# Three rounded matmuls in place of one plain f32 matmul in two input projections, rounding moved from VectorE to ScalarE, and a triangular inverse accumulated in PSUM

## The chip, the cores and the metric

The kernel runs on one core of a Trainium2 chip. The metric is the device time of one execution in microseconds. Engines are called as in the profile: PE (TensorE), DVE (VectorE), ACT (ScalarE), POOL (GpSimd), SP (SyncE, which here only issues DMAs).

## What is computed

Four transformer layers of width 1024 over 512 tokens, all in float32, with a context of 256 tokens. Cut to the parts that the change touches:

```python
# layer 1 (diff_fourier_mixer): q, k, v, f for the tokens, k and v for the context too
kv_c = h_ctx @ w_in[:, DA_W:3 * DA_W]
q, k, v, f = jnp.split(h_lat @ w_in, [DA_W, 2 * DA_W, 3 * DA_W], axis=-1)
...
# layer 2 (hyena_mixer)
u = dwconv3(h @ w_in, conv_w, conv_b)        # w_in is 1024 x 3072
...
# layer 3 (gated delta rule, 8 heads, chunks, two directions)
sol = lax.linalg.triangular_solve(lmat, rhs, left_side=True, lower=True, unit_diagonal=True)
```

Each of layers 1 and 2 ends in a gated convolutional FFN, each of layers 3 and 4 in a mixture of experts. Layer 4 has a short convolution as its mixer. Every mixer ends in an output projection.

## The kernel before, in words

The program is a list of 48 stages (`stages`). Each engine walks the list; after each stage it drains, adds one to `stage_end` and waits until all four have done so (L2782). Work of different stages never overlaps, except that SP loads weight slabs of 2 MB ahead of time into a ring of four slots (`slab`, `load_slab`); a slab's slot is free when its last user has called `used`.

**Rounded products.** A float32 product is made of three matmuls on operands rounded to the type fp32r: high x high, high x low, low x high (`three`, L508). `high` (L494) writes a rounded copy, `low` (L499) subtracts it from the original in place. `Parts` does this for a projection: the weights come in units of 128x1024 (one tile of 128 outputs), and the source is eight slices of 128x512. Before the change DVE makes the high parts of the units and of the source, and the low parts of the source (`cut_source`), POOL the low parts of the units (`make_low`), and PE waits for both in `product`. A ring of three units holds the high parts. It is used by `Project` (four stages), `FfnIn` (two), `ShortConv` (one), and in another form, by rows, by `FfnOut` (two). The high parts of the first three units precede those of the source on DVE. The experts' stages do their rounding on ACT already.

**AttentionIn** computes q, k, k of the context, v and f, 22 tiles, by plain f32 matmuls (L658); a plain f32 matmul stands in the trace as two records. After each of tiles 1 to 8 PE turns the halves for the rotary embedding (`swap`). DVE copies the tiles out, does the rotation, and between them (`BESIDE`) sums eight slabs of a `Modulation` (a matrix-vector product, L366 and L370, with short matmuls L382 on PE). The arena columns A_V, A_P and so on share the room of the later attention.

**HyenaIn** computes 24 tiles by plain f32 matmuls (L1269). ACT takes each out of PSUM with scale and bias (L1285), DVE adds the two other taps (`conv3`) and sums 12 side slabs. **HyenaFilter**, ahead of it, loads the table `hy_fwd` into Y_TAB, where it stays for **HyenaConv**, whose PE starts on it (L1338) after 32 transposes; `hy_back` is loaded over it later (L1319).

**DeltaHeads** runs eight heads, each with two directions, called lanes, of six 128x128 blocks. For each lane it inverts a unit triangular matrix by doubling: a level v takes the mask M of that level, A = M T (PE, L1793, into PSUM), copies A to SBUF (ACT, L1884), X = A TT (PE, L1803), TT -= X (DVE, L1974), and T = the 32x32 blockwise transpose of TT (DVE, L1977). M of the next level is a DVE product (`mask`, L1933). Up to level 4 T comes by the transpose, at level 5 (`WHOLE`) by its own product, and level 6 needs TT only. Then come six scan steps, beside which PE makes the next head's projections.

Of the kernel before, what the change touches and what calls it, by code (L numbers as in the profile page):

```python
# [27 lines left out]
P = 128  # L28
# [61 lines left out]
def _constants():  # L90
# [24 lines left out]
    masks = np.stack(levels, 1).reshape(P, 14 * P).astype(np.float32)  # L115
# [376 lines left out]
def high(c, dve, out, v):  # L492

    return dve.tensor_copy(c.rounded(out), v)  # L494
# [9 lines left out]

# [5 lines left out]
class Parts:  # L512

    def __init__(self, core, room, src, count):
        self.c, self.src = core, src
        self.src_high, self.ring = core.view(room, KD, T), room + KD * T
        self.cut, self.cut0 = core.shared("parts_cut", KD)  # L520
        self.made, self.made0 = core.shared("parts_high", count)
        self.low, self.low0 = core.shared("parts_low", count)

    def unit_high(self, u):
        return self.c.view(self.ring + KD * P * (u % UNITS), KD, P)

    def cut_source(self, dve):
        for k in range(KD):
            high(self.c, dve, self.src_high[:, k, :], self.src[:, k, :])
            dve.drain()  # L530
            low(self.c, dve, self.src[:, k, :], self.src_high[:, k, :]).then_inc(self.cut, 1)

    def make_high(self, dve, u, w, full, done):

        if u >= UNITS:
            dve.wait_ge(full, done + u - UNITS + 1)
        high(self.c, dve, self.unit_high(u), w).then_inc(self.made, 1)
# [4 lines left out]

    def product(self, pe, out, u, w):
        pe.wait_ge(self.low, self.low0 + u + 1)
        for k in range(KD):
            if u == 0:
                pe.wait_ge(self.cut, self.cut0 + k + 1)
            ins = three(self.c, pe, out, self.unit_high(u)[:, k, :], w[:, k, :], self.src_high[:, k, :], self.src[:, k, :],
                        k == 0, k == KD - 1)
        return ins  # L550


class Project(Stage):


    def __init__(self, core, w, src, gate, keep, room):
# [4 lines left out]
        self.parts = Parts(core, room, src, KD)  # L561
# [11 lines left out]
    def gpsimd(self, pool):  # L573
        for m in range(KD):
            self.parts.make_low(pool, m, self.unit(m))

    def vector(self, dve):
        c = self.c

        def make_high(m):  # L580
            if m < KD:
                if m % 4 == 0:
                    c.arrived(dve, self.n[m // 4])
                self.parts.make_high(dve, m, self.unit(m), self.full, self.base)

# [2301 lines left out]
```

## Time and profile before

| | us |
|---|---|
| three runs, median (lowest to highest) | 5049.75 (5049.54 to 5050.94) |
| the profiled execution, its time | 5045.87 |
| its span, first to last instruction | 5044.0 |

Its stages, cut at the last drain of each at L2782 (start and length in us): AttentionIn 107.00, 155.5; Project 485.12, 58.2; FfnIn 598.71, 280.3; FfnOut 879.01, 130.0; HyenaFilter 1035.63, 142.2; HyenaIn 1204.47, 182.0; HyenaConv 1386.43, 134.0; Project 1520.43, 57.5; FfnIn 1633.13, 289.3; FfnOut 1922.41, 128.9; DeltaHeads 2146.78, 1125.3; Project 3272.06, 58.3; experts 3412.69, 583.5; ShortConv 4045.18, 148.8; Project 4193.99, 57.5; experts 4333.84, 656.3. PE is busy for 82% of the span, DVE for 62%, ACT for 30%, POOL for 21%. Since the stages meet, the time is the sum of their lengths, and each length is read by itself: when its first matmul starts, how fast its tiles follow each other, and what trails the last one.

### The profile page before, as it was taken

To read this page: it belongs to the slowest core of one execution; us is meant where nothing else is said; L and a number is where in the kernel's file an instruction comes from. 1 tells how busy PE (TensorE), PEld (TensorE's weight loads), DVE (VectorE), ACT (ScalarE), POOL (GpSimd) and SP (SyncE) were. 2 spreads that over 40 slices of the span, in tenths; PEclk is the share of its full clock that TensorE was granted. 3 is DMA by queue.
4 is the path that set the end of the run, shared out by engine and by line. 5 is a ranking of instruction groups with operands and counts; after the bars stand their busy time and mean duration, and the time that the engine had idled before them with its cause. 6 is when DMAs were issued, how large, how long until landed. Compare 5 with 4: busy or idle time off the path is not lost. (4 is left out here: it accounts for less than half of the span.)

```text
span 5044.0 us, 50691 instructions
## 1 busy us (share of the span) xinstructions
PE 4138.2 (82%) x18124; PEld 3086.6 (61%) x18124; DVE 3127.2 (62%) x3756; ACT 1492.9 (30%) x1740; POOL 1049.8 (21%) x482
## 2 busy tenths in 40 slices
PE   4956799968986999678788888767999687599995
PEld 2523477723444777466666766656888566488884
DVE  5554577644644977355555455637999553699995
ACT  1031211011101110222222212106777400377773
POOL 0000243400001343000000000023555232155551
PEclk9977899969998999798988899778999898799997
DMA  4310155211510452100000000009999610699993
GB/s 170 134 67 18 50 174 193 76 55 67 205 45 34 150 170 90 33 17 17 17 17 17 17 17 6 28 19 348 363 359 370 223 67 2 247 377 359 369 357 121
DMA packets 372002, 689.22 MB, mean 137 GB/s; under 512 B 38311, under 2 KB 118311, under 8 KB 371304
## 3 DMA queue, kind: packets, MB, share of 16 engines
q1 hardware_dynamic: 327696, 639.79, 35.7%
q10 hardware_dynamic: 24888, 30.89, 1.8%
q0 software_dynamic: 19296, 16.94, 1.0%
q8 instruction: 75, 1.23, 0.1%
q14 instruction: 47, 0.39, 0.0%
HBM read 697.91 MB, written 41.00 MB: 146 GB/s over the span
## 5 line engine op out<-in xcount | busy, mean ns | idle before, releaser
L508 PE MATMUL psum<-work_rounded 128*128 128x512 f32 x3328 | 1089.2, 401 | 153.6 <-DVE fixed_rounded L499 70.9
L499 POOL TENSOR_TENSOR ring_rounded<-ring,work_rounded 128x1024 fp32r<-128x1024 f32 x188 | 460.9, 2454 | 3102.7 <-DVE work_rounded L494 3102.7
L508 PEld LDWEIGHTS psum<-work_rounded 128*128 128x128 f32 x3328 | 632.7, 192 | 314.8 <-issue 171.4
L508 PE MATMUL psum<-work_rounded,fixed_rounded 128*128 128x512 f32 x2304 | 683.1, 401 | 15.3 <-DVE fixed_rounded L2600 15.3
L499 DVE TENSOR_TENSOR ring_rounded<-ring,work_rounded 128x2048 fp32r<-128x2048 f32 x256 | 585.6, 2289 | 127.6 <-ACT work_rounded L2518 123.7
L508 PE MATMUL psum<-work_rounded,ring_rounded 128*128 128x512 f32 x1504 | 598.5, 398 | 0.0
L2518 ACT ACTIVATE work_rounded<-ring 128x2048 fp32r<-128x2048 f32 x256 | 490.8, 1919 | 272.3 <-PE psum L508 171.6
L508 PEld LDWEIGHTS psum<-work_rounded,fixed_rounded 128*128 128x128 f32 x2304 | 436.1, 189 | 119.7 <-DVE ring_rounded L499 12.0
L499 DVE TENSOR_TENSOR work_rounded<-work,work_rounded 128x2048 fp32r<-128x2048 f32 (+1 forms) x196 | 435.0, 2221 | 46.7 <-ACT work_rounded L2518 37.6
L476 ACT ACTIVATE work<-fixed 128x512 f32<-128x512 f32 (+1 forms) x120 | 64.6, 595 | 1119.9 <-DVE fixed L460 769.8
L508 PE MATMUL psum<-fixed_rounded,work_rounded 128*128 128x512 f32 x960 | 381.3, 397 | 0.0
L494 DVE CAST work_rounded<-ring 128x1024 fp32r<-128x1024 f32 x188 | 166.7, 893 | 274.8 <-PE psum L508 252.9
L508 PEld LDWEIGHTS psum<-work_rounded,ring_rounded 128*128 128x128 f32 x1504 | 287.9, 191 | 66.1
L508 PE MATMUL psum<-ring_rounded,fixed_rounded 128*128 128x512 f32 x768 | 306.9, 400 | 0.0
L370 DVE SCALAR_TENSOR_TENSOR work<-ring,fixed,work 128x512 f32<-128x512 f32 x392 | 289.5, 750 | 26.1 <-issue 1.3
L1674 PE MATMUL psum<-fixed,ring 128*128 128x512 f32 (+1 forms) x768 | 299.0, 525 | 0.4 <-DVEq L2782 0.4
L2380 POOL DMA_INDIRECT pair_rows<-work x66 | 173.5, 2629 | 561.3 <-DVE work L2610 559.3
L1793 PE MATMUL psum<-work 128*128 128x128 f32 x1152 | 166.6, 300 | 139.0 <-DVEq L1961 91.7
L2518 ACT ACTIVATE work_rounded<-work 128x2048 fp32r<-128x2048 f32 x128 | 245.3, 1919 | 101.3 <-PE psum L508 83.0
L1793 PEld LDWEIGHTS psum<-work 128*128 128x128 f32 x1152 | 149.4, 207 | 155.4 <-DVEq L1961 82.7
L508 PEld LDWEIGHTS psum<-fixed_rounded,work_rounded 128*128 128x128 f32 x960 | 184.1, 192 | 40.3
L968 ACT ACTIVATE work<-psum,fixed 128x512 f32<-128x512 f32 x88 | 68.5, 779 | 465.6 <-PE psum L508 465.6
(306 smaller groups left out, 6097.7 us busy)
## 6 DMA issues: line engine op xcount, KB each, us to landing
ring<-in_w SPq DMA_DIRECT2D x128, 2048.0 KB, 12.3
work<-in_w SPq DMA_DIRECT2D x64, 2048.0 KB, 11.9
ring<-in_mod_w SPq DMA_DIRECT2D x24, 2048.0 KB, 8.9
ring<-in_ada_w SPq DMA_DIRECT2D x24, 2048.0 KB, 7.9
ring<-in_ffn_w_in SPq DMA_DIRECT2D x44, 1024.0 KB, 7.6
ring<-in_ffn_w_out SPq DMA_DIRECT2D x10, 2048.0 KB, 7.7
ring<-in_w_in_a SPq DMA_DIRECT2D x32, 512.0 KB, 6.1
ring<-in_hy_w_in SPq DMA_DIRECT2D x6, 2048.0 KB, 9.4
```

The lines of the kernel that those rows point to most:

```text
L370: ins = dve.scalar_tensor_tensor(out=acc, in0=w[:, k, :], scalar=c.par(cond, k), in1=acc, op0=ALU.mult, op1=ALU.add)
L476: act.activation(c.view(self.scratch + 512 * k, t), src[:, k, :], ACT.Square).then_inc(s["squared"], 1)
L494: return dve.tensor_copy(c.rounded(out), v)
L499: return eng.tensor_tensor(c.rounded(v), v, c.rounded(v_high), ALU.subtract)
L508: ins = pe.matmul(out, c.rounded(w), c.rounded(x), start=(start and i == 0), stop=(stop and i == 2))
L968: act.activation(buf, c.ps[:, j % 7, :], ACT.Identity, scale=c.par(f"ffn_conv_w{i}1", m), bias=c.par(f"ffn_conv_b{i}", m)).then_inc(self.c ...
L1674: ins = pe.matmul(c.ps[:, 4 + i % 4, 0:n], self.slab_dst()[:, part, k, :], src[:, k, :], start=(k == 0), stop=(k == KD - 1))
L1793: ins = pe.matmul(c.pair(4 * l, KEYS)[:, P * t:P * t + P], M[:, t, :], T_[:, t, :], start=True, stop=True)
L2380: pool.indirect_dma_start(self.c.d["pair_rows"], bass.IndirectOffsetOnAxis(ap=self.si[:, b:b + 1].bitcast(U32), axis=0), self.y_sb[:, b, : ...
L2518: act.activation(c.rounded(self.unit_high(o, u)), self.unit_raw(o, u), ACT.Copy).then_inc(self.made, 1)
```

## The change

1. **AttentionIn and HyenaIn** use three rounded matmuls per product. AttentionIn gets 16 units in a ring of four, sources of both token sets (16 slices), and the order q, k, f, v; v's weights are four units that hold two k-slices each. HyenaIn gets a ring of two units in the context's room HC0 and puts the source's high parts over Y_TAB, so HyenaConv loads `hy_fwd` anew at its start.
2. **High parts by ACT** in every stage that used `Parts`, and in FfnOut. At the start of a stage ACT makes unit 0, slices 0 and 1, unit 1, and the other slices (`open_high`); DVE makes the low parts of unit 0 and the slices (`open_low`); POOL starts with unit 1.
3. **DeltaHeads**: the masks are stored negated, TT starts in PSUM (a matmul with the identity) and X is added there (`start=False`). DVE transposes straight from PSUM; ACT copies TT out of PSUM after it (24 copies per head in place of 12).

```diff
-masks = np.stack(levels, 1).reshape(P, 14 * P).astype(np.float32)
+masks = -np.stack(levels, 1).reshape(P, 14 * P).astype(np.float32)
...
-def high(c, dve, out, v):
-    return dve.tensor_copy(c.rounded(out), v)
+def high(c, act, out, v):
+    return act.activation(c.rounded(out), v, ACT.Copy)
...
+    def open_high(self, act, first, second):
+        high(self.c, act, self.unit_high(0), first).then_inc(self.made, 1)
+        for q, (v, v_high) in enumerate(self.src):
+            if q == 2:
+                high(self.c, act, self.unit_high(1), second).then_inc(self.made, 1)
+            high(self.c, act, v_high, v).then_inc(self.raised, 1)
+
+    def open_low(self, dve, first):
+        dve.wait_ge(self.made, self.made0 + 1)
+        low(self.c, dve, first, self.unit_high(0)).then_inc(self.cut, 1)
+        for q, (v, v_high) in enumerate(self.src):
+            dve.wait_ge(self.raised, self.raised0 + q + 1)
+            low(self.c, dve, v, v_high).then_inc(self.cut, 1)
...
 class AttentionIn(Stage):
-    BESIDE = [2, 5, 8, 13, 15, 18, 19, 20]
+    BESIDE = [2, 5, 8, 12, 14, 17, 19, 20]
...
+        for u in range(2, 16):                                   # ACT
+            if u in (4, 8, 12):
+                c.arrived(act, self.n["qkfv"[u // 4]])
+            if u >= 4:
+                act.wait_ge(self.full, self.base + (u - 4 if u < 8 else u) + 1)
+            high(c, act, self.unit_high(u), self.unit(u)).then_inc(self.parts.made, 1)
...
 class HyenaIn(Stage):
+        self.parts = Parts(core, [core.h], [core.view(Y_TAB, KD, T)], 24, unit_ring(core, HC0, 2))
...
         for j, m in enumerate(self.order):                       # ACT
             act.wait_ge(self.full, self.full0 + j + 1)
+            if j + 2 < 24:
+                if (j + 2) % 4 == 0:
+                    c.arrived(act, self.n[(j + 2) // 4])
+                self.parts.make_high(act, j + 2, self.unit(j + 2), None, 0)
...
 class HyenaConv(Stage):
+        act.dma_start(self.tab, self.c.d["hy_fwd"]...).then_inc(self.table, 16)
...
 class DeltaHeads(Stage):
+        for l in range(2):                                       # PE, ahead of the levels
+            self.wait(pe, h, "mt", l + 1)
+            for t in range(NTA):
+                pe.matmul(c.pair(4 * l + 2, KEYS)[:, P * t:P * t + P], ident, self.lane(l, L_TT, NTA, P)[:, t, :],
+                          start=(t % 4 == 0), stop=True, skip_group_check=True)
...
-                    ins = pe.matmul(c.pair(4 * l, KEYS)[:, P * t:P * t + P], A[:, t, :], TT[:, t, :], start=True, stop=True)
+                    ins = pe.matmul(c.pair(4 * l + 2, KEYS)[:, cols], A[:, t, :], TT[:, t, :], start=False, stop=True,
+                                    skip_group_check=True)
...
+            for l in range(2):                                   # ACT, after the two copies of A
+                if v < WHOLE:
+                    self.wait(act, h, "upd", 2 * v + 1 + l)
+                else:
+                    self.wait(act, h, "x", 2 * v - 1 + l)
+                act.activation(self.lane(l, L_TT, KEYS), c.pair(4 * l + 2, KEYS), ACT.Copy).then_inc(s["a_out"], 1)
...
-                dve.tensor_tensor(TT, TT, ax, ALU.subtract)      # DVE
-                if v < WHOLE:
-                    dve.drain()
-                    dve.transpose(self.lane(l, L_T, KEYS), self.lane(l, L_TT, KEYS))
+                if v < WHOLE:
+                    dve.transpose(self.lane(l, L_T, KEYS), c.pair(4 * l + 2, KEYS)).then_inc(s["upd"], 1)
```

## Rows read from the trace of the kernel before

**Rows 1.** Windows by stage: busy us of each engine (instructions), granted PE clock, DMA.
```profile
107.00:262.51 155.51, 154.37 (x432) 77.19 (x432) 75.57 (x112) 0.00 (x0) 0.00 (x0) 0.99 0.33 116
1204.47:1386.43 181.96, 179.82 (x480) 83.83 (x480) 109.80 (x155) 18.65 (x24) 0.00 (x0) 0.99 0.52 187
1633.13:1922.41 289.28, 268.35 (x1184) 216.07 (x1184) 236.63 (x303) 47.32 (x67) 106.33 (x44) 0.96 0.48 163
2146.78:3272.06 1125.28, 908.37 (x5344) 742.95 (x5344) 604.58 (x1072) 235.44 (x409) 0.00 (x0) 0.89 0.06 17
```

**Rows 2.** Windows: seven units of Project (168 matmuls), three tiles of HyenaIn (48).
```profile
503.13:541.97 38.84, 38.73 (x168) 31.23 (x167) 9.62 (x13) 0.00 (x0) 12.03 (x5) 1.00 0.16 54
1213.87:1234.51 20.64, 20.64 (x49) 8.88 (x47) 10.15 (x14) 2.33 (x3) 0.00 (x0) 1.00 0.21 80
```

**Rows 3.** Timeline of the opening of the first Project: start us, us, instruction.
```profile
485.28 4.04 DVE L494 CAST work_rounded<-ring 128x1024 fp32r<-128x1024 f32 x3 [0.19 <-ACTq L2782]
486.13 7.87 POOL L499 TENSOR_TENSOR ring_rounded<-ring,work_rounded 128x1024 fp32r<-128x1024 f32 x3 [485.69 <-DVE work_rounded L494]
491.88 2.66 DVE L499 TENSOR_TENSOR fixed_rounded<-fixed,work_rounded 128x512 fp32r<-128x512 f32 x1
494.69 0.77 PE L508 MATMUL psum<-work_rounded 128*128 128x512 f32 x1 [10.33 <-DVE fixed_rounded L499]
494.96 0.69 DVE L499 TENSOR_TENSOR fixed_rounded<-fixed,work_rounded 128x512 fp32r<-128x512 f32 x1
```

**Rows 4.** Groups by line, whole kernel: busy us, mean ns, idle before.
```profile
L2518 ACT ACTIVATE work_rounded<-ring 128x2048 fp32r<-128x2048 f32 x256 | 490.8, 1919 | 272.3 <-PE psum L508 171.6 <-DMA ring<-in_w 100.7
L499 DVE TENSOR_TENSOR ring_rounded<-ring,work_rounded 128x2048 fp32r<-128x2048 f32 x256 | 585.6, 2289 | 127.6 <-ACT work_rounded L2518 123.7
L499 POOL TENSOR_TENSOR ring_rounded<-ring,work_rounded 128x1024 fp32r<-128x1024 f32 x188 | 460.9, 2454 | 3102.7 <-DVE work_rounded L494 3102.7
L2528 ACT ACTIVATE fixed_rounded<-psum 128x512 fp32r<-128x512 f32 x128 | 68.3, 586 | 0.0
L464 DVE RECIPROCAL work<-work 128x512 f32<-128x512 f32 (+1 forms) x15 | 47.1, 3139 | 100.8 <-ACT work L478 100.8
```

**Rows 5.** Groups by line and form, first FfnOut.
```profile
L499 DVE TENSOR_TENSOR work_rounded<-work,work_rounded 128x512 fp32r<-128x512 f32 x22 | 59.9, 2723 | 1.6
```

**Rows 6.** Waits of PE, first FfnIn, then second: total us, times, longest us.
```profile
PE psum L508 <- POOL ring_rounded L499: 2.3, 1, 2.3
PE psum L508 <- POOL ring_rounded L499: 5.0, 3, 2.4
```

**Rows 7.** Timeline at the start of HyenaConv (its stage begins at 1386.43).
```profile
1384.04 2.00 SPq L245 DMA_DIRECT2D ring<-in_ffn_w_in  x2
1393.14 2.41 PE L1338 MATMUL psum<-fixed,work 128*128 128x512 f32 x5 [1.27 <-DVE fixed L1356]
```

**Rows 8.** DMA issues of HyenaConv: KB each, median us to landing.
```profile
work<-in_hy_back ACTq DMA_DIRECT2D x1, 2048.0 KB, 7.7
```

**Rows 9.** Timeline of DeltaHeads: first X, one level, start of the scan.
```profile
2365.50 0.95 DVE L1974 TENSOR_TENSOR work<-work,psum 128x768 f32<-128x768 f32 x1 [0.38 <-PE psum L1803]
...
2374.79 1.60 PE L1793 MATMUL psum<-work 128*128 128x128 f32 x12 [0.79 <-DVEq L1978]
2376.43 0.81 ACT L1884 ACTIVATE work<-psum 128x768 f32<-128x768 f32 x1 [4.26 <-PE psum L1793]
2378.36 2.84 PE L1803 MATMUL psum<-work 128*128 128x128 f32 x24
2379.90 0.95 DVE L1974 TENSOR_TENSOR work<-work,psum 128x768 f32<-128x768 f32 x1 [0.38 <-PE psum L1803]
2380.93 0.98 DVE L1977 STREAM_TRANSPOSE work<-work 128x768 f32<-128x768 f32 x1
2381.99 0.49 PE L1793 MATMUL psum<-work 128*128 128x128 f32 x2 [0.79 <-DVEq L1978]
...
2406.06 0.38 PE L1815 MATMUL psum<-work 128*128 128x128 f32 x1 [1.56 <-DVEq L1981]
```

More of the change, by code:

```diff
@@ L512, with __init__, make_high @@
 class Parts:
[L517 to L520, printed above, removed]
+    def __init__(self, core, src, src_high, count, units):
+        self.c = core
+        self.src = [(v[:, k, :], h[:, k, :]) for v, h in zip(src, src_high) for k in range(KD)]
+        self.units = units
+        self.raised, self.raised0 = core.shared("parts_raised", len(self.src))
+        self.cut, self.cut0 = core.shared("parts_cut", len(self.src) + 1)
         self.made, self.made0 = core.shared("parts_high", count)
-        self.low, self.low0 = core.shared("parts_low", count)
+        self.low, self.low0 = core.shared("parts_low", count - 1)
     def unit_high(self, u):
[L525 to L529, printed above, removed]
-            dve.drain()
[L531 to L537, printed above, removed]
+        return self.units[u % len(self.units)]
+    def open_high(self, act, first, second):
[10 more added lines that the diff above has]
+            low(self.c, dve, v, v_high).then_inc(self.cut, 1)
+    def make_high(self, act, u, w, full, done):
+        if full:
+            act.wait_ge(full, done)
+        high(self.c, act, self.unit_high(u), w).then_inc(self.made, 1)
     def make_low(self, pool, u, w):
@@ L667, in tensor, with gpsimd @@
             self.side.tensor_slab(pe, k)
+    def gpsimd(self, pool):
+        for u in range(1, 16):
+            w, w_high = self.unit(u), self.unit_high(u)
+            pool.wait_ge(self.parts.made, self.parts.made0 + u + 1)
+            low(self.c, pool, w, w_high).then_inc(self.parts.low, 1)
     def scalar(self, act):
@@ L1060, in tensor, with scalar @@
                 c.used(pe.drain(), self.n[kt // 4])
+    def scalar(self, act):
+        c = self.c
+        for kt in range(NF):
+            if kt % 4 == 0:
+                c.arrived(act, self.n[kt // 4])
+            if kt >= UNITS:
+                act.wait_ge(self.free, self.free0 + kt - UNITS + 1)
+            high(c, act, self.row_high(kt), self.row(kt)).then_inc(self.made, 1)
+            high(c, act, self.src_high(kt), self.src(kt)).then_inc(self.raised, 1)
     def vector(self, dve):
@@ L1262, in tensor @@
             n = self.n[j // 4]
-            if j % 4 == 0:
-                c.arrived(pe, n)
-            w = c.slot(n, KD, 512)
             if j >= 7:
                 pe.wait_ge(self.conv, self.conv0 + j - 6)
-            for k in range(KD):
-                ins = pe.matmul(c.ps[:, j % 7, :], w[:, k, P * (j % 4):P * (j % 4) + P], c.h[:, k, :],
-                                start=(k == 0), stop=(k == KD - 1))
-            ins.then_inc(self.full, 1)
+            self.parts.product(pe, c.ps[:, j % 7, :], j, self.unit(j)).then_inc(self.full, 1)
             if j % 4 == 3:
@@ L1286, in scalar, with gpsimd @@
                            bias=c.par("hy_conv_b", m)).then_inc(self.centre, 1)
+    def gpsimd(self, pool):
+        for j in range(1, 24):
+            self.parts.make_low(pool, j, self.unit(j))
     def vector(self, dve):
         c = self.c
+        self.parts.open_low(dve, self.unit(0))
         self.side.vector_slab(dve, 0)
@@ L1331, in tensor @@
         pe.wait_ge(self.turned_out, 8)
+        pe.wait_ge(self.table, 16)
         for i in range(8):
@@ L1421, in vector @@
         rows = T // GRID_W
-        def make_high(j):
-            if j < 24:
-                if j % 4 == 0:
-                    c.arrived(dve, self.n[j // 4])
-                self.parts.make_high(dve, j, self.unit(j), self.full, self.full0)
-        for j in range(UNITS):
-            make_high(j)
-        self.parts.cut_source(dve)
+        self.parts.open_low(dve, self.unit(0))
         for j in range(24):
```

185 lines of the change are left out of this document (113 added, 72 removed).

## The prediction, made before the changed kernel was run

> **What bounds the kernel now.** I read the drains at the stage ends first, since no two stages overlap; then the windows of the stages that the change touches, their timelines, and the waits of PE. In the windows [rows 1] PE is busy for 154.4 of 155.5 us in AttentionIn and 179.8 of 182.0 in HyenaIn: matmul time sets both. FfnIn is bound the same way (the second: 268.4 of 289.3), with an opening and a few waits. DeltaHeads is different: PE 908 of 1125 us, DVE 605, ACT 235, no engine full, so a chain of small steps sets it. The two rates of PE stand side by side [rows 2]: seven rounded products took 38.84 us, 5.55 each; three plain f32 tiles of HyenaIn took 20.64, 6.88 each, both at the full granted clock (1.00). The opening of a rounded stage is long [rows 3]: it begins at 485.12, PE's first matmul starts at 494.69, 9.6 us later.
>
> **The opening, and what blocks what.** The three casts of units and POOL's three low parts run into each other [rows 3]: POOL's three took 7.87 us, and DVE's first low part of the source, issued beside the last of them, 2.66, where the next, with POOL at rest, took 0.69. POOL's subtraction takes 2.45 [rows 4], and the DVE instruction behind it ends some 0.6 after it. FfnOut shows it in every row: 2.72 us for a 0.69 us subtraction [rows 5]. So a DVE operation on SBUF operands waits for POOL's whole instruction. The Trainium skill says so too (SBUF — State Buffer, section SBUF: two separate sides): the pair of ports shared by the two is an exclusive lock and the loser blocks fully. That rule speaks against the change, which keeps these subtractions on DVE and brings POOL into two stages that had none of it; I count the blocks below.
>
> Prices: ACT took 0.586 us for 128x512 and 1.919 for 128x2048 [rows 4], so a unit of 128x1024 lies between, by the line through both at 1.03. DVE's low part took 0.69 for 512 [rows 3] and 2.29 for 2048 [rows 4], so 1.22 for a unit. New opening, from the stage's start: ACT unit 0 until 1.3, slices 0 and 1 until 2.5, unit 1 until 3.5, the rest every 0.6 until 7.1, unit 2 until 8.1. DVE: unit 0 until 2.6, slice 0 at 3.3, slice 1 at 3.9. PE starts at 3.4 instead of 9.6. Then POOL has the ports for unit 1 until 6.3, DVE cuts slices 2 to 4 by 8.3, POOL takes unit 2 until 10.7, and DVE ends slice 7 at 12.7. Unit 0 is finished at 13.4. Before, it was finished at 18.0, where the window of the seven later units begins (503.13) [rows 2]. Gain 4.6 us for each of seven stages (four Project, two FfnIn, ShortConv). Bounds: none if POOL blocks DVE once per slice, 7 if it doesn't block at all (DVE then ends at 8.1). Granted clock: low PE speed at the start costs nothing extra, since PE waits for slices there.
>
> Four Projects: -18.4. ShortConv: -4.6. In steady state these stages stay at 5.55 per unit; the unit's high part on ACT (1.03) and low part on POOL (2.45) lie inside two products, and DVE's removed casts were hidden.
>
> **FfnIn.** PE waited for POOL's low parts 2.3 us in one stage and 5.0 in the other [rows 6]. These units were late because DVE made their high part only after a side slab; ACT doesn't sum slabs, so these waits go. DVE, relieved of 44 casts, ends its last slabs earlier and PE idles less before the last unit: 1 us (0 to 3) each. First -8 (4.6+2.3+1), second -11 (4.6+5.0+1). ACT gets 44 x 1.03 = 45 us on its 47 [rows 1]: 92 of 280. Queued behind the high part on ACT is the take-out from PSUM, 1 us later; PE has seven banks, so nobody waits.
>
> **FfnOut.** PE now needs ACT's row (1.3), then POOL's low part and, behind it, DVE's: 4.5 us from the start, against about 4.0: +0.5 each, +1 (0 to +3).
>
> **HyenaIn.** 24 tiles. From 6.88 to 5.55 saves 1.33 on 23 of them, -30.7. The first: before, PE began at once and the tile was over at 9.4 (1213.87, where the second window begins [rows 2]). Now there is one POOL block only, because the ring of two lets no unit 2 into the opening, so DVE ends slice 7 at 10.2 and the tile ends at 10.9: +1.5. The second weight slab needs the slot that DVE frees after side slab 0, now some 10 us later: +0.6. Sum -28.5. Cover: after product u ACT makes unit u+2 (1.03) and POOL its low part (2.45), with waits 3.8 us, inside product u+1 (5.55); that leaves 1.7. If it is gone, each us of excess costs 22. DVE is busy 110 us [rows 1], gets 7 us in the opening, and fits into 153.
>
> **HyenaConv.** `hy_fwd`, 2 MB, is issued at the start. A table of that size landed after 7.7 us with the queues free [rows 8]; here two loads of 1 MB have been issued 2 us before and PE starts on the table 6.7 us in [rows 7]. Alone it costs 1; sharing with these and what is still in flight, up to 10. I take +5.5.
>
> **AttentionIn.** 18 full tiles, the first set aside: 17 x 1.33 = -22.6. Four context tiles of 256 columns: half of a full product (2.8) against half of 6.88: -2.2; if the weight load (31.23/167 = 0.19 us [rows 2]) sets their pace instead, 4.5 each, +4.5 in all. Opening: unit 0 ends at 11.0; the tile before I take as in HyenaIn, 9.4: +1.6. DVE still has eight context slices to cut, and POOL's units 2 and 3 block it twice, until about 18; PE's first `swap` waits for its copy of tile 0, 2.5. A side slab is late by 0.6. For v, three slabs follow each other into the ring and four units have to pass POOL: +1.4. At the end DVE's last two side slabs are now behind PE: +2. Sum -17 (-25 to -5).
>
> **DeltaHeads.** Before, a level takes 7.20 us (2374.79 to 2381.99) [rows 9]: lane 0's product A, ACT's copy, X from 3.57 on, at 5.1 DVE's subtraction 0.95 and transpose 0.98. Lane 1 runs behind it, and X of lane 0 waits on PE for A of lane 1. Now, from the end of X of lane 0: transpose until 1.1; A from 1.1 to 2.7; the transpose of lane 1 is over at 2.4, so A of lane 1 runs from 2.5. ACT, in order: TT of lane 0 until 1.95, TT of lane 1 until 3.3, A of lane 0 until 4.1. X of lane 0 from 4.2 to 5.7. A level takes 5.7 to 5.8 us, set by ACT's queue. From the end of the first X to the first scan step: three levels 17.3; then 4.2, two X of double size 5.4, level 6 with its copies 6.6; 33.4. Before it was 40.6: DVE took up the first X at 2365.50, the scan began at 2406.06 [rows 9]. That is -7.2 a head, -57.5 for eight. The identity matmuls (2 x 1.4) fall where PE waits for DVE's preparation: 0. The transpose from PSUM isn't in the trace; nearest are the same from SBUF (0.98) and DVE's subtraction from PSUM, 0.95 [rows 9]. Bounds: 0.98, and their sum 1.93, at which the gain is gone. I take 0.98, for both rows stand near it. The Trainium skill (Perfetto Trace Analysis, section Optimizing Scalar/DVE Operations) puts a DVE access to PSUM 65 ns above one to SBUF; by that estimate 64 transposes would cost about 4 us more in all. The two rows here show no such difference.
>
> **Sum.** -18.4 -4.6 -8 -11 +1 -28.5 +5.5 -17 -57.5 = -138.5. The profiled execution's own time is 5045.87, its span 5044.0; the change falls inside the span, so 4907.4. The median of the runs shown is 3.9 above that execution, so 4911.
>
> **Rivals.**
> (a) The lock eats the openings: POOL and DVE alternate slice by slice, seven gains of 4.6 are gone: 4943. For it: every row of FfnOut. Against: POOL has only two units ready then. 10%.
> (b) The two new stages don't reach 5.55 per tile, since the ring (of two in HyenaIn) or a late slab makes PE wait, and the 44 us of both are gone: 4956. Against: 1.7 us of cover. 8%.
> (c) ACT's queue or a dearer transpose keeps the levels as long as before: the 57.5 go: 4969. 8%.
> (d) Slower than before: some DVE operations cost far more than a pass, as the reciprocal of 128x512 with 3.14 us [rows 4]. If a transpose from PSUM did, both lanes' stand on the chain in four levels of eight heads; beyond the 57.5 saved another 138.5 - 57.5 = 81 must be lost, 2.5 us in each of 32 levels, so at 0.98 + 0.95 + 1.25 = 3.2 us it decides. At 4.7 (the reciprocal's rate) about 5145. Against: it is a pass over the data like the one from SBUF. 2%.
> (e) More is gained: DVE's relief counts for 3 us in each FfnIn instead of 1 (-4), AttentionIn loses nothing at its seams (-8), the openings of seven stages are 2 us shorter (-14): 4885. 12%.
> The forecast itself, within 20 us: 60%.
>
> **How the numbers follow.** 4911 is the likeliest case; its own range is 4891 to 4931. With (a), most of (b) and half of (e) the range is 4880 to 4955; (c), (d) and the ends of the others are left out. Faster by over 0.2% (10 us, about what a measurement of this kernel tells from no change): everything but (d) and mishaps, 0.97; within: 0.01; slower: 0.02.
>
> **What would show it.** Rounded products 5.5 us apart in AttentionIn and HyenaIn; first matmul 3 to 4 us into a stage; stages of about 53.5 (Project), 272 and 278 (FfnIn), 153 (HyenaIn), 139 (AttentionIn and HyenaConv each), 1068 (DeltaHeads); levels of 5.7 us with ACT busy 3.2 of them. It would be wrong if PE waited for POOL in HyenaIn at every unit, if a transpose took much over 1 us, or if the changed rounding sent tokens to other experts and gave their stages another number of blocks.

## The result, and the profile after

| | us |
|---|---|
| before, median of 4 runs (lowest to highest) | 5049.65 (5048.97 to 5050.94) |
| after, median of 4 runs | 4928.84 (4925.53 to 4929.50) |
| ratio, 95% interval | 0.976 (0.974 to 0.978) |
| profiled execution after, its span | 4925.53, 4923.6 |

The forecast was 4911 (4880 to 4955), so the time lies inside the range, 18 us above its centre. The profiled executions stand 120.3 apart (5045.87 and 4925.53), where the sum was 138.5. The stages show that several terms missed in both directions. Lengths in us, cut at the last drain of each stage:

| stage | before | after | change | forecast |
|---|---|---|---|---|
| Project, four | 231.5 | 210.2 | -21.4 | -18.4 |
| ShortConv | 148.8 | 144.4 | -4.4 | -4.6 |
| first FfnIn | 280.3 | 277.0 | -3.3 | -8 |
| second FfnIn | 289.3 | 301.6 | **+12.3** | -11 |
| FfnOut, two | 258.9 | 260.4 | +1.5 | +1 |
| HyenaIn | 182.0 | 156.1 | -25.9 | -28.5 |
| HyenaConv | 134.0 | 140.1 | +6.1 | +5.5 |
| AttentionIn | 155.5 | 147.4 | -8.2 | -17 |
| DeltaHeads | 1125.3 | 1048.7 | -76.6 | -57.5 |
| all others | | | -0.4 | 0 |

Windows of the same four stages after, in the order of [rows 1]:

```profile
107.42:254.78 147.36, 131.66 (x608) 105.78 (x608) 107.92 (x129) 23.23 (x32) 40.21 (x15) 0.94 0.34 122
1189.04:1345.09 156.05, 149.61 (x672) 120.29 (x672) 133.50 (x164) 45.72 (x56) 48.65 (x23) 0.97 0.61 219
1593.17:1894.78 301.61, 273.96 (x1184) 220.83 (x1184) 219.53 (x252) 93.21 (x119) 110.46 (x43) 0.94 0.46 156
2118.29:3166.98 1048.69, 915.37 (x5536) 758.07 (x5536) 514.46 (x976) 309.75 (x505) 0.00 (x0) 0.90 0.07 18
```

Two things stand out. In AttentionIn PE was busy for all but 1.1 us before and now idles 15.7, of which the new opening is only a part. In the second FfnIn 52 casts have left DVE and one low part has come to it (303 instructions before, 252 now), yet DVE is busy only 17 us less (236.6 before, 219.5 now). The 52 casts alone took 51 us before (45.4 and 5.5 in the groups by line), so what is left has become dearer (the multiply-adds of the side slabs went from 81.7 to 118.1 us).

Windows of six units of Project and two tiles of HyenaIn, against [rows 2]: 5.61 and 5.62 each, at the full granted clock, as forecast (5.55).

```profile
489.42:523.09 33.67, 33.56 (x146) 26.98 (x144) 5.57 (x7) 5.32 (x5) 11.99 (x5) 1.00 0.18 63
1200.49:1211.73 11.24, 11.24 (x50) 9.04 (x49) 10.14 (x12) 3.45 (x4) 4.00 (x2) 1.00 0.37 135
```

Timeline of the opening of the first Project (from 476.67; PE's first matmul 3.2 us in, unit 0 over at 12.75), against [rows 3]:

```profile
476.70 1.06 ACT L494 ACTIVATE work_rounded<-ring 128x1024 fp32r<-128x1024 f32 x1 [51.95 <-DVEq L2870]
477.66 1.13 ACT L494 ACTIVATE work_rounded<-fixed 128x512 fp32r<-128x512 f32 x2
477.86 1.23 DVE L499 TENSOR_TENSOR ring_rounded<-ring,work_rounded 128x1024 fp32r<-128x1024 f32 x1 [1.22 <-ACT work_rounded L494]
...
479.00 9.27 DVE L499 TENSOR_TENSOR fixed_rounded<-fixed,work_rounded 128x512 fp32r<-128x512 f32 x8
...
479.88 2.65 POOL L499 TENSOR_TENSOR ring_rounded<-ring,work_rounded 128x1024 fp32r<-128x1024 f32 x1 [261.25 <-ACT work_rounded L494]
...
483.89 2.63 POOL L499 TENSOR_TENSOR ring_rounded<-ring,work_rounded 128x1024 fp32r<-128x1024 f32 x1 [1.36 <-ACT work_rounded L494]
```

DVE's eight slices take 9.27 us where eight at 0.69 would take 5.5: two blocks, one per POOL instruction, not one per slice. The estimated 1.03 for ACT's unit and 1.22 for DVE's are 1.06 and 1.23.

The row that the prediction did not look for is DVE's multiply-add of a side slab, read by its line in the whole kernel (shortest, median, longest ns), first before, then after:

```profile
L370 DVE SCALAR_TENSOR_TENSOR work<-ring,fixed,work x392: 743/751/754, 12.4 to 1906.0; 128x512 f32<-128x512 f32 x196
who waited for it (us, times):
  PE psum L382: 46.2, 5
```
```profile
L370 DVE SCALAR_TENSOR_TENSOR work<-ring,fixed,work x392: 739/752/2955, 12.5 to 1881.9; 128x512 f32<-128x512 f32 x196
who waited for it (us, times):
  PE psum L382: 71.9, 13
  PEld psum L382: 51.4, 12
```

Before, not one of 392 took over 0.754 us, and not one overlaps a POOL subtraction. After, the median is the same and the longest is 2.955. Counted in the trace, the 84 that overlap a POOL subtraction by over 0.1 us take 1.79 on average, the 308 others 0.75. Of the waits for the sums, 46 us stand in both kernels ahead of AttentionIn; the rest went from 0.2 to 25.8. The timeline of the second FfnIn shows one such sum and what hangs on it:

```profile
1633.98 14.40 DVE L370 SCALAR_TENSOR_TENSOR work<-ring,fixed,work 128x512 f32<-128x512 f32 x14
...
1637.67 2.94 POOL L499 TENSOR_TENSOR ring_rounded<-ring,work_rounded 128x1024 fp32r<-128x1024 f32 x1 [5.11 <-ACT work_rounded L494]
...
1640.97 2.39 POOL L499 TENSOR_TENSOR ring_rounded<-ring,work_rounded 128x1024 fp32r<-128x1024 f32 x1 [0.36 <-ACT work_rounded L494]
...
1647.77 3.57 PE L382 MATMUL psum<-fixed,work 128*128 128x1 f32 x16 [6.35 <-DVE work L370]
```

Fourteen multiply-adds take 14.40 us; before, the same fourteen took 10.35. PE has the short matmuls of that slab (L382) next in its order and stands 6.35 us in front of them. Sixteen of these matmuls ahead of the wait took 1.84 us, the sixteen behind it 3.57, at the lower of the two clock levels, 1.2 GHz (windows, granted clock 1.00 and 0.50):

```profile
1639.58:1641.42 1.84, 1.84 (x17) 1.75 (x15) 1.84 (x2) 1.58 (x2) 1.48 (x2) 1.00 0.00 0
1647.77:1651.34 3.57, 3.57 (x17) 3.57 (x17) 3.29 (x5) 0.63 (x1) 0.00 (x0) 0.50 0.49 129
```

The waits of PE in this stage, against the second row of [rows 6]:

```profile
PE psum L382 <- DVE work L370: 15.7, 6, 6.4
PE psum L505 <- issue: 2.1, 8, 0.3
PE psum L505 <- POOL ring_rounded L499: 0.8, 1, 0.8
```

The waits for POOL went from 5.0 to 0.8, as forecast. In their place are 15.7 us of waits for DVE. PE's busy time for the same 1184 instructions also rose, 268.4 to 274.0, at a granted clock of 0.94 for the stage (0.96 before); behind the longest wait it was as low as the rows above show.

The third slab of AttentionIn shows the same. The seven multiply-adds of the slab before it, with POOL at rest, took 5.71 us. Its own seven took 11.57, three of them 2.67 to 2.74 each beside a subtraction of POOL, and PE's wait of 6.74 us ends with them:

```profile
177.69 11.57 DVE L370 SCALAR_TENSOR_TENSOR work<-ring,fixed,work 128x512 f32<-128x512 f32 x7
```

DeltaHeads, timeline of one level, against [rows 9]; the first and the last row shown are the same copy of two levels, 5.56 us apart:

```profile
2333.07 0.81 ACT L1976 ACTIVATE work<-psum 128x768 f32<-128x768 f32 x1 [1.75 <-DVE work L2063]
2333.19 2.85 PE L1879 MATMUL psum<-work 128*128 128x128 f32 x24
2333.39 0.98 DVE L2063 STREAM_TRANSPOSE work<-psum 128x768 f32<-128x768 f32 x1 [0.36 <-PE psum L1889]
2334.41 0.81 ACT L1976 ACTIVATE work<-psum 128x768 f32<-128x768 f32 x1 [0.53 <-DVE work L2063]
2334.73 0.96 DVE L2025 TENSOR_TENSOR work<-work 128x768 f32<-128x768 f32 x1 [0.36 <-PE psum L1879]
2335.11 0.81 ACT L1970 ACTIVATE work<-psum 128x768 f32<-128x768 f32 x1
2335.97 2.94 PE L1889 MATMUL psum<-work 128*128 128x128 f32 x24
...
2338.63 0.81 ACT L1976 ACTIVATE work<-psum 128x768 f32<-128x768 f32 x1 [1.75 <-DVE work L2063]
```

L1976 is ACT's copy of TT, L1970 that of A. The copy of A starts at 2335.11, with no idle time before it: it queues behind the copy of TT of lane 1, while the product A of lane 0 was there at 2334.73, where DVE starts the mask that waits for that product. PE's X (L1889) starts when the copy is over. The transpose from PSUM takes 0.98.

At the start of HyenaConv [rows 7] PE starts on the table 10.8 us into the stage where it was 6.7, and the issue row gives its landing, against [rows 8]:

```profile
1355.92 1.19 PE L1417 MATMUL psum<-fixed,work 128*128 128x512 f32 x1 [4.25 <-DMA work<-in_hy_fwd]
```
```profile
work<-in_hy_fwd ACTq DMA_DIRECT2D x1, 2048.0 KB, 10.7
```

### The profile page after: what moved, and what is told of

Same layout as the page of the kernel before. It is cut to its first block and busy times, and to the rows that moved or that the text cites. A ratio compares the mean times of both kernels' runs of the same rounds, so it can differ in the third digit from the quotient of the medians.

```text
span 4923.6 us, 51743 instructions
## 1 busy us (share of the span) xinstructions
PE 4100.6 (83%) x18684; PEld 3172.6 (64%) x18684; DVE 2940.2 (60%) x3405; ACT 1857.4 (38%) x2188; POOL 1129.3 (23%) x513
## 5 line engine op out<-in xcount | busy, mean ns | idle before, releaser
L505 PE MATMUL psum<-work_rounded 128*128 128x512 f32 x3504 | 1159.6, 401 | 125.8 <-DVE fixed_rounded L499 65.7
L505 PE MATMUL psum<-work_rounded,fixed_rounded 128*128 128x512 f32 x2544 | 782.1, 402 | 32.5 <-DVE fixed_rounded L2688 16.0
L505 PE MATMUL psum<-work_rounded,ring_rounded 128*128 128x512 f32 (+1 forms) x1824 | 724.9, 397 | 0.0
L499 DVE TENSOR_TENSOR ring_rounded<-ring,work_rounded 128x2048 fp32r<-128x2048 f32 (+1 forms) x264 | 595.5, 2257 | 150.8 <-ACT work_rounded L2606 127.0
L494 ACT ACTIVATE work_rounded<-ring 128x1024 fp32r<-128x1024 f32 x204 | 215.8, 1058 | 985.6 <-PE psum L505 712.4
L505 PE MATMUL psum<-fixed_rounded,work_rounded 128*128 128x512 f32 (+1 forms) x1088 | 430.0, 395 | 0.0
L370 DVE SCALAR_TENSOR_TENSOR work<-ring,fixed,work 128x512 f32<-128x512 f32 x392 | 376.6, 972 | 25.8 <-issue 0.9
L1754 PEld LDWEIGHTS psum<-fixed,ring 128*128 128x128 f32 x768 | 136.8, 192 | 88.8 <-issue 83.5
L2462 POOL DMA_INDIRECT fixed<-h_rows,work x64 | 171.2, 2674 | 54.6 <-POOL work L2459 54.6
L968 DVE SCALAR_TENSOR_TENSOR work<-psum,fixed,work 128x511 f32<-128x511 f32 x112 | 83.7, 747 | 162.6 <-ACT work L1040 147.4
## 6 DMA issues: line engine op xcount, KB each, us to landing
ring<-in_w SPq DMA_DIRECT2D x128, 2048.0 KB, 13.4
```

The source lines that it names most:

```text
L370: ins = dve.scalar_tensor_tensor(out=acc, in0=w[:, k, :], scalar=c.par(cond, k), in1=acc, op0=ALU.mult, op1=ALU.add)
L494: return act.activation(c.rounded(out), v, ACT.Copy)
L499: return eng.tensor_tensor(c.rounded(v), v, c.rounded(v_high), ALU.subtract)
L505: ins = pe.matmul(out, c.rounded(w), c.rounded(x), start=(start and i == 0), stop=(stop and i == 2))
L968: dve.scalar_tensor_tensor(out=out[:, 1:n], in0=u[:, 0:n - 1], scalar=w0, in1=out[:, 1:n], op0=ALU.mult, op1=ALU.add)
L1754: ins = pe.matmul(c.ps[:, 4 + i % 4, 0:n], self.slab_dst()[:, part, k, :], src[:, k, :], start=(k == 0), stop=(k == KD - 1))
```

## The experiments

The theory after the result: DVE's side-slab sums are blocked by POOL's subtractions, PE waits for the sums, and this cost the second FfnIn 23 us and AttentionIn some 7. Rivals: the rounding work itself has become slower on ACT, or PE waits for weight slabs.

**1. No POOL in FfnIn.** POOL only passes its signal on, and PE reads the high part of units 1 to 43 in place of the low part; the low parts of these weights are left out of the computation, so its results are other numbers.

```diff
-            self.parts.product(pe, c.ps[:, j % 7, :], j, self.unit(j)).then_inc(self.full, 1)
+            self.parts.product(pe, c.ps[:, j % 7, :], j, self.parts.unit_high(j) if j else self.unit(j)).then_inc(self.full, 1)
...
-            self.parts.make_low(pool, j, self.unit(j))
+            pool.wait_ge(self.parts.made, self.parts.made0 + j + 1)
+            pool.drain().then_inc(self.parts.low, 1)
```

> The changed kernel, but in both FfnIn stages POOL's subtraction is left out for units 1 to 43, and PE reads the high part in the place of the low part (the product loses these low parts). Everything on ACT, DVE, PE and the DMA queue stays. Lock theory (POOL's low parts now run beside DVE's side slabs and block them): the slab's multiply-adds (L370), 972 ns on the mean over the changed kernel, fall back to 750 in FfnIn, PE's waits for slab sums (15.7 us in the second FfnIn) fall under 2, and the stages take 270 to 273 us (from 277.0) and 272 to 277 us (from 301.6). Queue theory (ACT makes the high part ahead of taking a tile out of PSUM, and stands waiting for weight slabs, so that DVE starts its work late): L370 may fall, but the waits for the sums stay above 10 us and the second FfnIn stays above 293.

Measured: the FfnIn stages take 269.5 and 274.0 us (270 to 273 and 272 to 277 expected). Group by line and form in the second:

```profile
L370 DVE SCALAR_TENSOR_TENSOR work<-ring,fixed,work 128x512 f32<-128x512 f32 x112 | 81.7, 750 | 6.3
```

With POOL at rest the 112 take 0.750 on average, none over 0.754, and PE waits for no sum. ACT's rounding takes 46.6 us for the 44 units as after, so it isn't the cause. ACT waits 10.5 us for weight slabs (18.3 after), but in neither kernel does a wait of PE end with a slab or with ACT. In AttentionIn, where this edit leaves POOL at work, PE's wait for the third slab stays at 6.8. The whole time, 4825.7, can't be compared: the other numbers send tokens to other experts, whose two stages became 35 us shorter each.

**2. High parts of FfnIn by DVE again.** After the opening, DVE makes the high part of unit j+3 ahead of its work on tile j.

```diff
-            make_high(j + UNITS, self.full0 + j + 1)                      # ACT
...
+            if j + UNITS < 2 * NF:                                        # DVE, before tile j
...
+                dve.wait_ge(self.full, self.full0 + j + 1)
+                dve.tensor_copy(c.rounded(self.parts.unit_high(j + UNITS)), self.unit(j + UNITS)).then_inc(self.parts.made, 1)
```

> The changed kernel, but in FfnIn the high parts from unit 3 on are made by DVE again, ahead of each tile's taps, as before the change; the new opening stays, and so does POOL's subtraction. Lock theory: a side slab on DVE now holds back the next high part and with it POOL, so slabs and POOL's work no longer overlap: L370 back to 750 ns, the two FfnIn near the times before less the opening's 5.2 us, 275 and 284. Queue theory: the same, by way of ACT's free queue; so this run does not tell them apart alone, it tells what giving the edit back is worth. If neither holds, the second FfnIn stays near 301.

Measured: 4915.97 (one run); 274.6 and 284.3. Second FfnIn, group and waits of PE:

```profile
L370 DVE SCALAR_TENSOR_TENSOR work<-ring,fixed,work 128x512 f32<-128x512 f32 x112 | 81.7, 750 | 6.6 <-issue 0.4
```
```profile
PE psum L505 <- POOL ring_rounded L499: 4.8, 3, 2.3
```

That is the interlock that the kernel before had without saying so. While DVE sums a slab it makes no high part, so POOL has no low part to make and doesn't take the ports from it: in this stage none of the 112 multiply-adds overlaps a POOL subtraction, neither before nor here, and after 33 do (by over 0.1 us). It costs PE 4.8 us of waits for POOL; the free ACT costs it 15.7 of waits for DVE.

**3. The DeltaHeads change alone**, on the kernel before: its class and the negated masks, nothing else.

```diff
-masks = np.stack(levels, 1).reshape(P, 14 * P).astype(np.float32)
+masks = -np.stack(levels, 1).reshape(P, 14 * P).astype(np.float32)
...
 class DeltaHeads(Stage):          # the whole class as in the change
```

> The kernel before with the change of DeltaHeads alone (masks negated, inverse accumulated in PSUM). If the parts add up by stage: DeltaHeads 1048 to 1050 us (from 1125.3), the whole 5049.7 - 76.6 = 4973. If part of the 76.6 comes from elsewhere (the state in which earlier stages leave the PE clock or the slabs), DeltaHeads stays above 1056, where the forecast's 57.5 plus a few would put it.

Measured: 4969.53 (4966.56 to 4972.91, 4 runs), ratio to before 0.985 (0.983 to 0.986). DeltaHeads takes 1047.6, and the whole is 3 us below the 4973 expected. So the gain of this stage doesn't hang on the other parts of the change.

**4. Two orders on ACT.** In AttentionIn ACT's five DMA issues go behind the opening's rounding. In DeltaHeads ACT copies TT and A by turns, lane by lane, instead of A, A, TT, TT.

```diff
-        act.dma_start(c.view(A_ROPE, 2 * T), c.d["rope"]).then_inc(self.table, 16)
-        ...                                                      # and the four of L727
         c.arrived(act, self.n["q"])
         self.parts.open_high(act, self.unit(0), self.unit(1))
+        act.dma_start(c.view(A_ROPE, 2 * T), c.d["rope"]).then_inc(self.table, 16)
+        ...
...
+        copy_a(1, 0)
+        copy_a(1, 1)
         for v in range(1, LEVELS):
             for l in range(2):
-                ...                                              # copy A
-            for l in range(2):
-                ...                                              # copy TT
+                copy_tt(v, l)
+                if v + 1 < LEVELS:
+                    copy_a(v + 1, l)
```

> Two edits of order in stages that don't touch. AttentionIn: ACT issues its five DMAs after the opening's high parts in place of ahead of them. I hold that these issues delay the first high part by 3 us: the first matmul comes 3.3 us into the stage in place of 6.1, the stage takes 144 to 145 us (from 147.4). Rival: the late swap or a side slab decides anyway, and it stays at 147. DeltaHeads: ACT copies TT of lane 0, A of lane 0, TT of lane 1, A of lane 1, in place of both TT ahead of both A. If ACT's queue sets the level (5.57 us), it falls to 5.35, where PE's 48 matmul records (24 x 0.223) fill it, and the stage by 5 to 9 us to 1040 to 1044; if the chain over DVE sets it, nothing changes (1048.7).

Measured: 4909.68 (one run). Windows of the two stages:

```profile
107.21:251.97 144.76, 131.91 (x608) 106.01 (x608) 108.79 (x129) 23.24 (x32) 40.19 (x15) 0.94 0.36 125
2119.43:3151.31 1031.88, 896.11 (x5536) 743.16 (x5536) 513.82 (x976) 304.69 (x505) 0.00 (x0) 0.92 0.07 18
```

AttentionIn gains 2.6: in the kernel after, the first rounding came 3 us into the stage, behind the issues (timeline):

```profile
107.50 0.35 ACTq L723 DMA_DIRECT2D work<-in_rope  x1
...
109.72 0.62 ACTq L727 DMA_DIRECT2D work<-in_da_lam_k  x1
110.39 1.06 ACT L494 ACTIVATE work_rounded<-ring 128x1024 fp32r<-128x1024 f32 x1 [2.99 <-issue]
```

DeltaHeads gains 16.8, more than the 5 to 9 expected. The levels alone account for 0.78 us a head, 6.2 in all (from the first A of a head to its scan, counted in the trace: 38.45 and 37.67 on average). The rest lies in stretches that the edit doesn't touch, and goes with the granted clock. The seven stretches from the last scan step of a head to the next head's first A are 7.9 us shorter in sum (0.83 to 0.87 in four of them, where after none is above 0.81), and the last head's scan is 3.0 shorter (1.00 against 0.74). Over the stage the clock is 0.92 against 0.90, and PE's 5536 instructions take 896 us against 915.

**5. PE takes the sums later.** In FfnIn the short matmuls of a slab come one weight slab (four units) later (the first slab's stay), those of the last two slabs behind the last unit. In AttentionIn those of the third slab come two tiles later.

```diff
-            if i - 3 in self.BESIDE:                                     # AttentionIn
-                self.side.tensor_slab(pe, self.BESIDE.index(i - 3))
+            beside = [self.BESIDE[0] + 3, self.BESIDE[1] + 3, 13] + [b + 3 for b in self.BESIDE[3:]]
+            if i in beside:
+                self.side.tensor_slab(pe, beside.index(i))
...                                                                       # FfnIn
             if q == 2 and s:
-                for q_side in ([0] if s == 1 else []) + self.beside[s - 1]:
-                    self.side.tensor_slab(pe, q_side)
+                self.side.tensor_slab(pe, s - 1)
...
+        for q_side in (10, 11):
+            self.side.tensor_slab(pe, q_side)
```

> The changed kernel; in FfnIn PE takes each side slab's sum one group of four tiles later (the last two after the last tile), in AttentionIn the third one two tiles later. Nothing is done to POOL or to the slabs. Lock theory: L370 stays slow beside POOL (FfnIn mean above 850 ns), but since PE reached the sums too early, its waits for them (15.7 us in the second FfnIn, 7.5 in AttentionIn) and the low clock behind them go: first FfnIn 270 to 272 (from 277.0), second 278 to 284 (from 301.6), AttentionIn 141 to 142 (from 147.4). Rival: DVE is short of time in the second FfnIn with the slabs of 16 us (a group of four tiles costs it 26 to 28 us against PE's 24.4), PE then waits for PSUM banks in place of the sums, and the stage stays above 290. HyenaIn, not touched, comes out at 156 or at 162, as it did without an edit of its own in e2.

Measured: 4888.20 (one run). FfnIn 270.9 and 274.7, AttentionIn 142.7 (141 to 142 expected); the second FfnIn is better than the 278 to 284 expected. DVE's sums stay dear in every kernel with this edit. In the second FfnIn of experiment 9 below:

```profile
L370 DVE SCALAR_TENSOR_TENSOR work<-ring,fixed,work 128x512 f32<-128x512 f32 x112 | 112.1, 1021 | 6.3
```

but in both FfnIn PE no longer waits for any of them. So POOL's subtractions are the cause of the late sums (experiment 1), and PE's place for them is what made it cost time: moved, the two stages are 6.1 and 26.9 us shorter.

**6 and 7. HyenaIn.** In experiments 1 and 2 this stage took 162.2 and 162.1 us, though nothing in it had been touched; after, in 4 and in 5 it took 155.8 to 156.1. Counted in the trace, unit 20, the first of the last weight slab, starts 6.8 us behind unit 19 in the short form, 9.9 (experiment 2) and 10.4 (experiment 1) in the long one. Its matmuls then start over a stretch of 8.2 and 8.0 us in place of 5.5. ACT's longest wait for a weight slab, after and in experiment 2:

```profile
1314.07 1.06 ACT L494 ACTIVATE fixed_rounded<-ring 128x1024 fp32r<-128x1024 f32 x1 [7.67 <-DMA ring<-in_hy_w_in]
```
```profile
1315.14 1.06 ACT L494 ACTIVATE fixed_rounded<-ring 128x1024 fp32r<-128x1024 f32 x1 [11.02 <-DMA ring<-in_hy_w_in]
```

Experiment 6 moves each weight slab one side slab ahead in SP's order; experiment 7 lets ACT take the tile out of PSUM before it waits for the slab.

```diff
             self.n.append(core.slab(k_slab(w, P * self.order[4 * s], P * self.order[4 * s] + 512)))
-            side.add_slab()
-            if s < 5:
-                side.add_slab()
+            if s:
+                side.add_slab()
+            side.add_slab()
```

> As the kernel of late sums, and in HyenaIn each weight slab is loaded ahead of the two side slabs that now precede it in SP's queue. My theory of the 6 us between 156 and 162: ACT waits for a late weight slab (32.5 us in all in the changed kernel, 36 where the stage took 162) with tiles in PSUM that it has not taken out, and at unit 20 PE runs out of banks. Then the waits of ACT for in_hy_w_in fall under 12 us, no unit steps over 6.6 us, and HyenaIn takes 154 to 156. If the cause lies with the units' low parts or DVE, unit 20 still steps 9 to 10 us and the stage takes 160 to 162.

> As the kernel of late sums, and in HyenaIn ACT takes a tile out of PSUM before it waits for the next weight slab (the slabs' order is as in the changed kernel). If the stall at unit 20 comes from tiles not taken out: HyenaIn 155 to 157. If it comes from the slab itself being late for the unit's high and low part: unit 20 still steps 9 to 10 us, 160 to 163.

Measured: 4889.71 and 4896.60 (one run each); HyenaIn 162.0 and 162.5. The first is a miss, the second falls under its second alternative. In 6 PE's wait at unit 20 is gone: it starts 6.1 us behind unit 19, and the last unit ends earlier. ACT still waits 17.1 us for weight slabs, where under 12 was expected. But a side slab now sits in the slot of the fifth weight slab, and another comes behind it, so the end of the stage waits for them. Waits in HyenaIn of experiment 6:

```profile
PE psum L382 <- DVE work L370: 5.4, 1, 5.4
DVE work L366 <- DMA ring<-in_ada_w: 4.6, 1, 4.6
```

In 7 unit 20 starts 10.4 us behind unit 19. PE waits 4.6 us there for POOL's low part of the unit, where in experiment 2 the 4.0 us of wait ended with DVE's tap, so tiles left in PSUM are not what holds it: the slab itself came late.

**8. All of it**: experiments 4, 5 and 6 together.

> All edits that keep the computation: late sums (FfnIn, AttentionIn), weight slabs first in HyenaIn, ACT's DMAs after the opening in AttentionIn, ACT's copies of A and TT in turn in DeltaHeads. If the stages add up: against the changed kernel AttentionIn -8 (of it 2.6 measured), FfnIn -6 and -20, HyenaIn -1, DeltaHeads -10 to -17: about 4928 - 48 = 4880 us. If savings are given back at the next wait, 4895 or more.

Measured: 4875.86 (4873.87 to 4879.64, 5 runs), ratio 0.966 (0.965 to 0.968); some 4880 was expected. HyenaIn takes 162.2 again, with the same wait at its end (5.4 us) as in 6.

**9 and 10. HyenaIn once more**, both with experiments 4 and 5. In 9 the slabs come in the old order, and DVE sums each side slab one unit earlier, which frees the slot that the last weight slab needs. In 10 HyenaIn is as it was.

```diff
-            if j % 2 == 1 and j < 22:
+            if j % 2 == 0 and j < 22:
                 self.side.vector_slab(dve, j // 2 + 1)
```

> The edits of the late sums, of the early ACT work in AttentionIn and of the DeltaHeads order, and in HyenaIn the old order of slabs, but DVE sums each side slab one unit earlier. Theory: the last weight slab lands in the slot that DVE frees after side slab 8; with that slab summed one unit (some 6 us) earlier the weight slab is there in time, unit 20 follows in 6.1 us in place of 6.8 to 10.4, and the last side slab, in the slot of the fifth weight slab, is summed before the last unit ends: HyenaIn 154 to 156, whole kernel 4868 to 4872. Rival: the loads go at the pace of the 16 DMA engines, so the slab lands when it did, and the stage stays at 156 or 162: whole kernel 4870 or 4876.

> The same without any edit in HyenaIn. Theory that the stage has two lengths, set by whether the last weight slab comes in front of unit 20 or 3.6 us behind it: 156 or 162, nothing between, so the kernel is at 4870 or 4876. Rival: the 162 of the kernel with all edits comes from the shifted slabs alone (its last side slab is late); then this kernel shows 156 and 4870.

Measured: 4866.61 (4863.26 to 4869.65, 5 runs), ratio 0.964 (0.963 to 0.965), the fastest kernel of the study; and 4871.31 (4869.08 to 4873.00, 5 runs), ratio 0.965 (0.964 to 0.966). HyenaIn takes 155.0 and 155.9. Windows of HyenaIn and of the second FfnIn in 9:

```profile
1175.52:1330.52 155.00, 149.62 (x672) 120.33 (x672) 141.84 (x164) 46.06 (x56) 49.81 (x23) 0.97 0.62 220
1577.45:1852.04 274.59, 264.27 (x1184) 213.50 (x1184) 218.21 (x252) 92.67 (x119) 109.70 (x43) 0.98 0.51 171
```

DVE is busier in HyenaIn (141.8 against 133.5), for its sums now meet POOL more often, and the stage is a little shorter all the same. That makes 0.9 us of the 5.5 between the two profiled executions. The rest stands in stages whose code doesn't differ, so no more than that is shown for the edit. Experiment 10 decides for the rival in its expectation: the 162.2 of experiment 8 came from the shifted slabs. That the untouched stage is 6 us longer in experiments 1 and 2 is another matter, seen in one profile each. The late slab is seen there; why it lands later isn't known.

## Why the prediction was right, and where it was wrong

**The openings** (forecast -4.6 each): right in mechanism and nearly in size. Project gained 5.2 to 5.4; PE started at 3.2 (forecast 3.4) and ended unit 0 at 12.75 (13.4). Rival (a) falls: two blocks for two POOL instructions. The rule of the Trainium skill (SBUF — State Buffer, section SBUF: two separate sides) says that the loser blocks fully. The trace of after agrees: of DVE's eight slices six took 0.69 us, and the two that met POOL's instructions of 2.65 and 2.63 took 2.78 and 2.87.

**FfnIn, the step that failed**: "ACT doesn't sum slabs, so these waits go. DVE, relieved of 44 casts, ends its last slabs earlier and PE idles less before the last unit". The first half held (5.0 to 0.8 us). The second did not: I applied the lock to subtractions only, and the multiply-adds of a side slab fall under it too (0.75 alone, 1.79 on average beside POOL). The same section of the Trainium skill names DVE operations with two SBUF inputs, and a multiply-add of a side slab is one; the trace of after agrees. The trace of before already held a sign: DVE's product of two SBUF operands in FfnIn (L1005, 128x512) took 1.32 us in the 40 that met a POOL subtraction and 0.69 in the 4 that didn't. What I didn't see is that DVE's order of work had kept its sums apart from POOL. It cost 23 us against the forecast in the second FfnIn, 5 in the first. The second suffers more: it waits 15.7 us for sums, the first 2.6. Its slabs take 14 multiply-adds each, the first's 7, and after unit 6 PE takes two slabs at once; the wait there was the longest (6.35), and the granted clock fell behind it.

**AttentionIn** (forecast -17, measured -8.2): two things were missed. ACT's five DMA issues stand ahead of the rounding: 2.6 us (experiment 4). The sum behind tile 11 costs PE 6.7 us: 4.65 of the stage (experiment 5). That POOL makes this sum late is read from the trace of after; no run took POOL away in this stage. With both mended the stage takes 138.5 to 139.9 (experiments 8 to 10) against 138.5 forecast, so the other terms hold in their sum. The late side slab was in it with 0.6. One term was slightly off as worked out: four context tiles at 2.8 in place of 3.44 save 2.6, not 2.2. In rival (b) the two stages' gains add up to 45.5, not 44.

**HyenaIn** (forecast -28.5, measured -25.9): the rate of 5.6 stands, and PE waits for POOL 1.7 us in all, so rival (b) falls. The 2.6 missing lie at the seams: unit 1 starts 11.4 us in (10.9 forecast), those waits for POOL are 1.7, and each weight slab is awaited by ACT (32.5 us in five waits, of which only the excess over the cover reaches PE). The cover was thinner than I counted at one place, the last weight slab.

**HyenaConv** (+5.5, measured +6.1): PE waited 4.25 us for the table, which landed after 10.7; before, a table of the size took 7.7 [rows 8].

**FfnOut** (+1, measured +1.5) and **ShortConv** (-4.6, measured -4.4): as forecast.

**DeltaHeads** (forecast -57.5, measured -76.6): the mechanism was right, its size too small. The level takes 5.57 us (5.7 to 5.8 forecast), set by ACT's queue, as said. From the first A of a head to its scan, counted in both traces, it was 46.9 us and is 38.45, so 8.5 a head and 68 in eight, where I had 7.2 and 57.5. The rest, some 9 us, fits the granted clock (0.89 to 0.90). The stretch from the last scan step of a head to the next head's first A, in which only the identity matmuls were added, went from 55.7 us at 0.73 to between 53.5 and 54.4 at 0.81 and 0.75 in the later heads, 8.4 us over all seven. Where the clock was alike in both (0.78), it took 53.5 us in both, so the identity matmuls, put at 0, cost nothing there. Why the clock comes out higher there isn't shown. Rivals (c) and (d) fall with one row: the transpose from PSUM takes 0.98 us, as from SBUF. The 65 ns more for PSUM, estimated from the figures of the Trainium skill (Perfetto Trace Analysis, section Optimizing Scalar/DVE Operations), aren't borne out for this operation: 983 ns in the median of 64 of them against 978 from SBUF.

Rival (e) did not come in the form it had: the openings were 0.7 us shorter than forecast, not 2, and DVE's relief had the opposite sign. The total came out near the forecast because DeltaHeads and the openings gave 22 us more, and FfnIn, AttentionIn and HyenaIn 39 less. The two errors have nothing to do with each other; that they nearly cancel is luck.

## What to carry to other kernels

Before work is moved from one engine to a free one, ask what its old place kept apart: here DVE's own casts held POOL back while DVE was summing, and the free engine let the two meet. When a helper engine's results come late but nobody needs them soon, move the consumer in PE's order, not the helper: taking the sums four units later gave 33 us in two stages with the sums nearly as dear as before. Issues of DMAs ahead of an engine's first compute instruction count as part of a stage's opening, and two copies in one queue are worth ordering by who waits for them.

## What the runs showed of the hardware that was not expected

- DVE's multiply-add with all operands in SBUF took 751 ns alone and up to 2955 beside a POOL subtraction of 128x1024. DVE's taps, the same operation with one operand in PSUM, weren't slowed at all beside the same POOL instructions, though 39 of these 44 met one. By their line in the first FfnIn (L968, shortest, median, longest ns):

```profile
L968 DVE SCALAR_TENSOR_TENSOR work<-psum,fixed,work x44: 739/750/752, 605.9 to 860.1; 128x511 f32<-128x511 f32 x44
```

- In HyenaIn of experiment 2 PE started unit 20 some 3.5 us late (9.9 us behind unit 19, where 6.4 is usual), and that unit took 8.2 us where the others take 5.5: mostly at the lower of the two levels, 1.2 GHz. Windows of that unit and of the stretch behind it, granted clock 0.59 and 1.00:

```profile
1317.94:1325.93 7.99, 7.41 (x20) 5.96 (x21) 7.35 (x11) 0.54 (x1) 2.39 (x2) 0.59 1.05 396
1327.00:1332.40 5.40, 5.40 (x29) 4.53 (x28) 1.50 (x2) 1.73 (x2) 2.00 (x1) 1.00 0.94 320
```

So the wait cost about 2.7 us more than it lasted.

- POOL's subtraction of 128x1024 took 2.00 us in the median of 23 in HyenaIn after, and 2.41 in the 196 of the other stages, at the same shape and type. The operands lie in other buffers there; why it is faster isn't known. It widened the cover of 1.7 us that the prediction counted by some 0.4.
